# Rolling up five stages of a layer-stack kernel, and moving one addition of the retention from GpSimd to TensorE

## The chip, the cores and the metric

The kernel runs on one core of a Trainium2 chip. A core has TensorE (PE in the profile, its weight loads as PEld), VectorE (DVE), ScalarE (ACT), GpSimd (POOL) and SyncE (SP), which here only issues transfers from HBM to the on-chip memory. The metric is the device time of one execution in microseconds.

## The reference

The program computes three blocks on a sequence of 256 tokens and 1024 features, in float32: a block with three kinds of attention and a convolutional FFN, a block with stick-breaking and block attention and a SwiGLU FFN, and a block with retention and a SwiGLU FFN. What the change touches is this much of it: the two SwiGLU FFNs, the first block's FFN, and the group norm over each retention head.

```python
h = rmsnorm(x, ffn_pre_norm[l])                                   # stages "up", "down"
u = causal_depthwise_conv(h @ w_up[l], conv_w[l], conv_b[l])
gate, up = jnp.split(u, 2, axis=-1)
y = (jax.nn.gelu(gate, approximate=True) * up) @ w_down[l]
...
# the two later FFNs, SwiGLU: stages "gu0", "dn0" and "gu1", "dn1"
...
# retention (stage "ret_in"): 4 heads, 512 values each; every head's output is
# normalised over its 512 values, which needs their sum of squares per token
```

## The kernel before, in words

All activations lie transposed: 128 features on the partitions, 256 tokens along the free dimension, 8 such tiles for 1024 features. Every weight matrix is cut into chunks of up to 128 x 2048 elements. A chunk is loaded by SyncE into one of four raw slots; ScalarE rounds it to fp32r (`w_hi`, L802), VectorE computes the remainder (`w_lo`, L2219), each in two halves into one of two slots; and TensorE multiplies three times per tile (L1474 to L1476: hi x hi, lo x hi, hi x lo). So a chunk of the stages up, gu0 and gu1 is 16 tiles or 48 matmuls of 256 columns, and a chunk of dn0 and dn1 is 11 tiles or 33 matmuls. There are 22 chunks in up, gu0 and gu1 each, and 16 in dn0 and dn1 each. Finished chunks lie in two PSUM banks (`lin`); a bank is given free through the semaphores `lin_free`.

Each engine has its own instruction stream, written in the order in which it runs, and the streams meet only in semaphores. In gu0 ScalarE leaves the gate half of a chunk (L1330), GpSimd and VectorE form the products (L2585 reads the up half and gives the bank free), and VectorE in between multiplies pieces of a large conditioning matrix (L2323, with the accumulator read, and L2326, which writes a column of `mod`).

The helper `steps(eng, n, lead, tail, body)` runs a stage's chunks on an engine. Before the change it ignores `lead` and `tail` and calls `body(Step(c))` for every chunk, so all chunks are written out in the stream. The class `Step` can also carry a loop register `i`; its method `n(f)` then gives a value that grows by `f(j + 4) - f(j)` per trip, used for the semaphore values, the columns and the addresses.

In the retention, ScalarE squares the four 128-value pieces of a head's output (L1421, `sq`, 1024 columns). GpSimd adds the upper 512 columns to the lower (L762), and then columns 256 to 511 to columns 0 to 255 (L765). TensorE then sums over the partitions with two 128x1 matmuls (`ret_sums`, L2160), one for each half of the tokens, placed in the middle of a chunk. VectorE reads the sums (L2873).

Of the kernel before, what the change touches and what calls it, by code (L numbers as in the profile page):

```python
# [18 lines left out]
ALU = mybir.AluOpType  # L19

P = 128
S = 256
# [17 lines left out]
UNROLL = 4  # L40
# [144 lines left out]

def steps(eng, n, lead, tail, body):

    for c in range(n):
        body(Step(c))


# [22 lines left out]
def scaled_before(norm):  # L214

    return sum(norm_tiles(i) for i in range(norm))
# [24 lines left out]
def deferred_before(norm):  # L241
    return sum(i < norm for i in DEFERRED)


def additions(norm, n):

    if norm == PRE:
        return 0
    if norm in DEFERRED:
        return 5 if norm == L0F else 6  # L250
    return max(n - 1 - 3, 0)
# [28 lines left out]
def build(nc, dram):  # L280
    ctx = ExitStack()
    with ctx:
        def sb(name, n, dt=F32, parts=P):
            return ctx.enter_context(nc.sbuf_tensor(name, [parts, n], dt))

        def sem(name):
            return ctx.enter_context(nc.semaphore(name))
# [9 lines left out]
        ident, ones = sb("ident", P), sb("ones", S)  # L297
# [13 lines left out]
        def parts(table, end=ADA0 - D):  # L311
            at, out = 0, {}
            for name, n in table:
                out[name] = arena[:, at:at + n]
                at += n
            assert at <= end, (at, end)
            return out

        e0, a1, ff, a2, rt = parts(EARLY), parts(ATT1), parts(FFN), parts(ATT2), parts(RET, ARENA)
# [19 lines left out]
        ssum = sco[0][:, 0:6]  # L339
# [6 lines left out]
        def spread_bank(i, g):  # L346
# [36 lines left out]
        ret_rot, ret_s, ret_inner, v_centred, ret_o, ret_sq, ret_added, ret_ssum, ret_ms, ret_root, ret_diag, ret_rbc = (  # L383
            sem(n) for n in ("ret_rot", "ret_s", "ret_inner", "v_centred", "ret_o", "ret_sq", "ret_added", "ret_ssum", "ret_ms",
                             "ret_root", "ret_diag", "ret_rbc"))
# [17 lines left out]
        def v3(ap, n):  # L403
            return ap.rearrange("p (a b) -> p a b", a=n)
# [17 lines left out]
        for i, layer, which in ((L0, 0, 0), (L0F, 0, 3), (L1, 1, 0), (L1F, 1, 3)):  # L422
            NORM[i] = (x[:, :], e0["sq"], e0["y"],
                       lambda k, i=i: gscale[:, 8 * (L0, L0F, L1, L1F).index(i) + k:8 * (L0, L0F, L1, L1F).index(i) + k + 1],
# [11 lines left out]
        def rbc_copy(i):  # L436
            return arena[:, SETTLED_AT[i]:SETTLED_AT[i] + S]
# [5 lines left out]
        def z_cut(i, k, lo_, n=S):  # L443

            parts_ = Z_PARTS[i]
            first, _, at = parts_[0] if len(parts_) == 1 or k < parts_[0][1] else parts_[1]
            return Z_IN[i][lo_][:, bass.ds((k - first) * ZW + at, n)]
# [5 lines left out]
        def shifts(i, part):  # L453
            which = (L0, L0F, L1, L1F).index(i)
            at, (first, end, _) = 48 * (which // 2) + 24 * (which % 2), Z_PARTS[i][part]
            return mod[:, at + first:at + end].unsqueeze(2).to_broadcast([P, end - first, ZW - S])
# [14 lines left out]
        def settled_tile(i, c, b):  # L471
            return settled_chunk(i, c)[:, b * ZW:b * ZW + S]
# [220 lines left out]
        @block.gpsimd  # L693
        def _(pool):
            added = [0]

            def add_squares(i):

                sq, k0 = NORM[i][1], 0
                for n in NORM_GROUPS[i]:  # L700
                    acc = sq[:, k0 * S:(k0 + 1) * S]
                    for k in range(k0 + 1, k0 + 1 + additions(i, n)):
                        pool.wait_ge(sq_ready, scaled_before(i) + k + 1)
                        if k > k0 + 1:

                            pool.wait_ge(sq_added, added[0])
                        nc.gpsimd.tensor_tensor(acc, acc, sq[:, k * S:(k + 1) * S], ALU.add).then_inc(sq_added, 1)  # L707
                        added[0] += 1
                    k0 += n

            def hidden(step):
                j = step.j
                at, cut = S * (j % 2), bass.ds(step.n(lambda c: c * S), S)
                hid = ff["hid"][:, at:at + S]

                pool.wait_ge(gelu_ready, step.n(lambda c: c + 1))
                nc.gpsimd.tensor_tensor(hid, ff["u"][:, 2 * at + S:2 * at + 2 * S], ff["g"][:, at:at + S], ALU.mult)\
                    .then_inc(hid_ready, 1)
                pool.wait_ge(hid_hh, step.n(lambda c: c + 1))
                nc.gpsimd.tensor_tensor(hid_lo[:, cut], hid, hid_hi[:, cut].bitcast(F32), ALU.subtract).then_inc(hid_tiles, 1)  # L720

            def remainder(base):
                def one(step):
                    j = step.j
                    pool.wait_ge(hid_hh, step.n(lambda c: base + c + 1))
                    cut = bass.ds(step.n(lambda c: c * S), S)
                    nc.gpsimd.tensor_tensor(hid_lo[:, cut], ff["hid"][:, S * (j % 2):S * (j % 2) + S], hid_hi[:, cut].bitcast(F32),  # L727
                                            ALU.subtract).then_inc(hid_tiles, 1)
                return one

            pool.wait_ge(band_ready, 1)
            pool.dma_start(dram["band"], band).then_inc(band_out, 16)
            pool.wait_ge(band_out, 16)
            pool.dma_start(dram["band_rows"], dram["band_repeat"]).then_inc(band_out, 16)
            pool.wait_ge(band_out, 32)
            pool.dma_start(v3(a1["bias"], 8), dram["band_skew"]).then_inc(bias_in, 16)
            def settle(i):

                pool.wait_ge(rbc_copied, deferred_before(i) + 1)
                ph = PH[AHEAD[i]]  # L740
                for c in range(DEFERRED_CHUNKS):
                    for b in range(2):
                        if b == 0:
                            pool.wait_ge(first_left, DEFERRED_CHUNKS * deferred_before(i) + c + 1)
                        else:
                            pool.wait_ge(lin_free[(ph.unit0 + c) % 2], (ph.unit0 + c) // 2 + 1)
                        nc.gpsimd.tensor_tensor(settled_tile(i, c, b), settled_tile(i, c, b), rbc_copy(i), ALU.mult)\  # L747
                            .then_inc(settled, 1)

            for i in range(len(NORM_GROUPS)):  # L750
                if i != PRE and NORM_GROUPS[i]:
                    add_squares(i)
                if i in DEFERRED:
                    settle(i)
                if i in (L0F, L1F):

                    steps(pool, FT, 2, 0, remainder(FT if i == L0F else 2 * FT))
                if i == L1:

                    for h in range(RET_H):  # L760
                        pool.wait_ge(ret_sq, 2 * h + 2)
                        nc.gpsimd.tensor_tensor(rt["sq"][:, 0:512], rt["sq"][:, 0:512], rt["sq"][:, 512:1024], ALU.add)\  # L762
                            .then_inc(ret_added, 1)
                        pool.wait_ge(ret_added, 2 * h + 1)
                        nc.gpsimd.tensor_tensor(rt["sq"][:, 0:S], rt["sq"][:, 0:S], rt["sq"][:, S:2 * S], ALU.add).then_inc(ret_added, 1)  # L765
                if i == FFNPRE:

                    steps(pool, PH["up"].n, 2, 1, hidden)
                if i == FINAL:
                    pool.wait_ge(x_gains, DT)  # L770
                    pool.wait_ge(rbc_copied, len(DEFERRED) + 1)
                    for k in range(FINAL_SPLIT, DT):
                        cut = slice(k * S, (k + 1) * S)
                        nc.gpsimd.tensor_tensor(e0["y"][:, cut], e0["y"][:, cut], e0["sq"][:, 0:S], ALU.mult).then_inc(pool_tiles, 1)
# [696 lines left out]
        def _(pe):  # L1471
# [682 lines left out]
            def ret_sums(h):  # L2154


                pe.wait_ge(ret_inner, RET_H)
                pe.wait_ge(ret_added, 2 * h + 2)
                for r in range(2):
                    ins = nc.tensor.matmul(ssum[:, r:r + 1], rt["sq"][:, r * P:r * P + P], ones[:, 0:1],  # L2160
                                           start=r == 0, stop=r == 1, skip_group_check=True)
                ins.then_inc(ret_ssum, 1)

            def ret_spread(h):
# [980 lines left out]
```

## Time and profile before

| | us |
|---|---|
| median of 3 runs | 1054.75 (1052.81 to 1055.11) |
| the profiled execution | 1054.75 |
| its span, first to last instruction | 1053.0 |
| TensorE busy | 1027.0 |
| VectorE busy | 804.9 |
| ScalarE busy | 594.6 |
| GpSimd busy | 161.6 |

Busy means that at least one instruction of the engine was under way; matmuls overlap each other, so their durations add up to more than the span. Register instructions, waits and branches are not counted as busy. The stages lie in the span about as follows: up from 160 to 269 us, down to 331, gu0 from 460 to 589, dn0 to 652, gu1 from 850 to 982, dn1 to 1040.

### The profile page before, as it was taken

How to read it: one execution, taken by the hardware profiler on the slowest of the kernel's cores; microseconds unless marked ns; L12 is line 12 of the kernel's file. 1: busy time of each engine (PE TensorE's matmuls, PEld its weight loads, DVE VectorE, ACT ScalarE, POOL GpSimd, SP SyncE). 2: the span in 40 equal slices, each digit the busy share in tenths (PEclk: the TensorE clock that was granted, in tenths of full speed). 3: DMA queues.
4: the chain of work that ended last, by engine and by line, in shares of the span. 5: the costliest groups of instructions: out<-in, count | busy, mean ns of one | idle time of the engine just before them, and what ended most of it. 6: DMA issues, size and time to landing. Idle time of an engine off the chain costs nothing.

```text
span 1053.0 us, 19187 instructions
## 1 busy us (share of the span) xinstructions
PE 1027.0 (98%) x7842; PEld 975.0 (93%) x7842; DVE 804.9 (76%) x1380; ACT 594.6 (56%) x1029; POOL 161.6 (15%) x168
## 2 busy tenths in 40 slices
PE   7999999999999999999999999999999999999997
PEld 6987798999888997899999999998899999999997
DVE  5867789999997987588999688885668566674443
ACT  6686667666546675675444445543556466544443
POOL 0000033323201200024212001200110114111010
PEclk8999999999999999999999999999999999999999
DMA  9642336777695543157998788554444536774441
GB/s 369 248 143 98 103 131 227 301 273 284 256 391 228 165 152 125 74 207 278 375 370 340 283 326 306 170 193 160 126 155 142 218 122 226 278 278 150 166 166 40
DMA packets 33988, 227.49 MB, mean 216 GB/s; under 512 B 3779, under 2 KB 4076, under 8 KB 10220
## 3 DMA queue, kind: packets, MB, share of 16 engines
q1 hardware_dynamic: 33452, 223.63, 57.9%
q0 software_dynamic: 448, 2.63, 0.6%
q8 instruction: 62, 1.02, 0.4%
q14 instruction: 26, 0.21, 0.1%
HBM read 225.19 MB, written 2.63 MB: 216 GB/s over the span
## 4 chain that ended last, share of the span: by engine, by line
PE 80%; DVE 12%; ACT 5%; issue 1%; DMA 0%; POOL 0%; POOLq 0%; SPq 0%; ACTq 0%; DVEq 0%
PE psum L1474 20%; PE psum L1476 20%; PE psum L1475 20%; DVE w_lo L2219 5%; PE psum L1539 2%; PE psum L1542 2%; PE psum L1541 2%; PE psum L1883 2%; PE psum L1885 2%; PE psum L1884 2%; ACT w_hi L802 2%; DVE arena L2522 1%; DVE arena L2323 1%; DVE hid_lo L2304 1%; PE psum L2149 1%
## 5 line engine op out<-in xcount | busy, mean ns | idle before, releaser
L2219 DVE TENSOR_TENSOR w_lo<-raw,w_hi 128x1024 fp32r<-128x1024 f32 (+1 forms) x342 | 389.5, 1161 | 148.2 <-ACT w_hi L802 143.3
L802 ACT ACTIVATE w_hi<-raw 128x1024 fp32r<-128x1024 f32 (+1 forms) x342 | 335.4, 996 | 209.7 <-PE psum L1476 157.7
L1474 PE MATMUL psum<-h_hi,w_hi 128*128 128x256 f32 (+1 forms) x1144 | 325.5, 285 | 7.6 <-DVE w_lo L2219 3.0
L1475 PE MATMUL psum<-h_lo,w_hi 128*128 128x256 f32 (+1 forms) x1144 | 321.1, 281 | 0.0
L1476 PE MATMUL psum<-h_hi,w_lo 128*128 128x256 f32 (+1 forms) x1144 | 320.6, 280 | 0.0
L1474 PE MATMUL psum<-hid_hi,w_hi 128*128 128x256 f32 (+1 forms) x952 | 270.9, 285 | 0.6 <-DVE w_lo L2219 0.4
L1475 PE MATMUL psum<-hid_lo,w_hi 128*128 128x256 f32 (+1 forms) x952 | 268.1, 282 | 0.0
L1476 PE MATMUL psum<-hid_hi,w_lo 128*128 128x256 f32 (+1 forms) x952 | 268.1, 282 | 0.0
L1474 PEld LDWEIGHTS psum<-h_hi,w_hi 128*128 128x128 f32 x1144 | 215.3, 188 | 10.7 <-DVE w_lo L2219 5.4
L1475 PEld LDWEIGHTS psum<-h_lo,w_hi 128*128 128x128 f32 x1144 | 216.2, 189 | 0.7 <-issue 0.7
L1476 PEld LDWEIGHTS psum<-h_hi,w_lo 128*128 128x128 f32 x1144 | 215.9, 189 | 0.0
L1474 PEld LDWEIGHTS psum<-hid_hi,w_hi 128*128 128x128 f32 x952 | 179.4, 188 | 2.1 <-DVE w_lo L2219 1.2
L1475 PEld LDWEIGHTS psum<-hid_lo,w_hi 128*128 128x128 f32 x952 | 179.5, 189 | 0.0
L1476 PEld LDWEIGHTS psum<-hid_hi,w_lo 128*128 128x128 f32 x952 | 179.3, 188 | 0.0
L2323 DVE CUSTOM_DVE_ANT_0 arena<-arena 128x1024 f32<-128x1024 f32 x96 | 128.0, 1370 | 0.7 <-DMA arena<-in_ada 0.4
L707 POOL TENSOR_TENSOR arena<-arena 128x256 f32<-128x256 f32 x33 | 28.3, 857 | 427.7 <-ACT arena L1263 255.7
L1154 ACT ACTIVATE hid_hi<-arena 128x256 fp32r<-128x256 f32 x60 | 25.1, 418 | 100.2 <-DVE arena L2585 75.0
L727 POOL TENSOR_TENSOR hid_lo<-arena,hid_hi 128x256 fp32r<-128x256 f32 x44 | 41.9, 952 | 169.2 <-ACT hid_hi L1154 157.0
L747 POOL TENSOR_TENSOR arena<-arena 128x256 f32<-128x256 f32 x30 | 36.2, 1228 | 77.5 <-ACT arena L1052 64.7
L1883 PE MATMUL psum<-w_hi,hid_hi 128*128 128x512 f32 x88 | 34.8, 396 | 0.0
L1884 PE MATMUL psum<-w_hi,hid_lo 128*128 128x512 f32 x88 | 34.7, 395 | 0.0
L1885 PE MATMUL psum<-w_lo,hid_hi 128*128 128x512 f32 x88 | 34.7, 395 | 0.0
(294 smaller groups left out, 1215.7 us busy)
## 6 DMA issues: line engine op xcount, KB each, us to landing
arena<-in_ada SPq DMA_DIRECT2D x48, 1024.0 KB, 6.3
raw<-in_gu SPq DMA_DIRECT2D x44, 1024.0 KB, 6.9
raw<-in_ret_in SPq DMA_DIRECT2D x24, 1024.0 KB, 4.9
raw<-in_up SPq DMA_DIRECT2D x22, 1024.0 KB, 4.9
raw<-in_dn SPq DMA_DIRECT2D x32, 704.0 KB, 4.2
raw<-in_qkv SPq DMA_DIRECT2D x12, 1024.0 KB, 5.0
raw<-in_down SPq DMA_DIRECT2D x11, 1024.0 KB, 8.3
raw<-in_ret_o SPq DMA_DIRECT2D x8, 1024.0 KB, 4.8
```

What stands on the lines that cost most here:

```text
L707: nc.gpsimd.tensor_tensor(acc, acc, sq[:, k * S:(k + 1) * S], ALU.add).then_inc(sq_added, 1)
L727: nc.gpsimd.tensor_tensor(hid_lo[:, cut], ff["hid"][:, S * (j % 2):S * (j % 2) + S], hid_hi[:, cut].bitcast(F32), ALU.subtract).then_inc(h ...
L747: nc.gpsimd.tensor_tensor(settled_tile(i, c, b), settled_tile(i, c, b), rbc_copy(i), ALU.mult)\
L802: nc.scalar.activation(w_hi[chunk % SPLIT_SLOTS][:, a:b], raw[chunk % RAW_SLOTS][:, a:b], ACT.Copy)\
L1474: nc.tensor.matmul(out, w[0], hc, start=start, stop=False, skip_group_check=True)
L1475: nc.tensor.matmul(out, w[0], lc, start=False, stop=False, skip_group_check=True)
L1476: return nc.tensor.matmul(out, w[1], hc, start=False, stop=stop, skip_group_check=True)
L1883: nc.tensor.matmul(bank[:, :], hid_hi[:, t:t + P], whi[:, w], start=c == 0 and k == 0, stop=False, skip_group_check=True)
L1884: nc.tensor.matmul(bank[:, :], hid_lo[:, t:t + P], whi[:, w], start=False, stop=False, skip_group_check=True)
L1885: ins = nc.tensor.matmul(bank[:, :], hid_hi[:, t:t + P], wlo[:, w], start=False, stop=last and k == 1, skip_group_check=True)
L2219: tt(w_lo[s][:, a:b], raw[chunk % RAW_SLOTS][:, a:b], w_hi[s][:, a:b].bitcast(F32), ALU.subtract)\
L2323: ins = nc.vector.tensor_tensor_reduce(w, w, cond_silu, 1.0, 0.0, ALU.mult, ALU.add, sums[:, b:b + 1])
```

## The change

It has two parts. `steps` now writes out only the first `lead` chunks and what is left at the end; in between it puts four chunks (UNROLL) into a loop that runs `trips` times. On TensorE this gives 3 trips each in up, gu0, gu1 and dn0, and 2 in dn1. VectorE gets 3 trips in up and gu0 and 2 in dn0 and dn1; ScalarE 3 in up and gu0 and 2 in dn0, gu1 and dn1; SyncE and GpSimd have such loops as well. The order of the work on each engine is the same. In the second part GpSimd's second addition per head goes, and TensorE sums four pieces with four 128x1 matmuls.

```diff
 def steps(eng, n, lead, tail, body):
 
-    for c in range(n):
+    lead = min(lead, n)
+    trips = (n - lead - tail) // UNROLL
+    if trips < 2:
+        trips = 0
+    for c in range(lead):
+        body(Step(c))
+    if trips:
+        with eng.Fori(0, trips) as i:
+            for j in range(UNROLL):
+                body(Step(lead + j, i))
+    for c in range(lead + trips * UNROLL, n):
         body(Step(c))
...
                         nc.gpsimd.tensor_tensor(rt["sq"][:, 0:512], rt["sq"][:, 0:512], rt["sq"][:, 512:1024], ALU.add)\
                             .then_inc(ret_added, 1)
-                        pool.wait_ge(ret_added, 2 * h + 1)
-                        nc.gpsimd.tensor_tensor(rt["sq"][:, 0:S], rt["sq"][:, 0:S], rt["sq"][:, S:2 * S], ALU.add).then_inc(ret_added, 1)
...
-                pe.wait_ge(ret_added, 2 * h + 2)
-                for r in range(2):
-                    ins = nc.tensor.matmul(ssum[:, r:r + 1], rt["sq"][:, r * P:r * P + P], ones[:, 0:1],
-                                           start=r == 0, stop=r == 1, skip_group_check=True)
+                pe.wait_ge(ret_added, h + 1)
+                for f in range(2):
+                    for r in range(2):
+                        ins = nc.tensor.matmul(ssum[:, r:r + 1], rt["sq"][:, f * S + r * P:f * S + r * P + P], ones[:, 0:1],
+                                               start=f == 0 and r == 0, stop=f == 1 and r == 1, skip_group_check=True)
```

TensorE's stream where the loop of gu0 begins, now. The loop's first chunk starts behind the branch; before, the matmuls stand here without anything between them.

```order
L1484 MATMUL psum<-h_hi,w_lo 128x256
L195 UNCONDITIONAL_BRANCH
L195 ISA
L408 ISA [waits split_ready]
L1482 MATMUL psum<-h_hi,w_hi 128x256 [waits lin_free1]
L1483 MATMUL psum<-h_lo,w_hi 128x256
```

And where the same loop ends, 192 matmuls later, now:

```order
L1484 MATMUL psum<-h_hi,w_lo 128x256
L195 REGISTER_ALU
L195 COMPARE_AND_BRANCH
L1482 MATMUL psum<-h_hi,w_hi 128x256 [waits lin_free1,split_ready]
```

Two register instructions and a branch have come between the matmuls, and some register instructions stand between tiles inside the loop.

VectorE's stream in gu0, one chunk, before:

```order
L2585 TENSOR_TENSOR arena<-psum,arena 128x256 [waits hid_tiles,gelu_ready]
L2323 ISA arena,ada_sums<-arena 128x1024 [waits ada_in1]
L2323 ISA ada_sums 128x1
L2323 ISA arena,ada_sums<-arena 128x1024
L2323 ISA ada_sums 128x1
L2326 TENSOR_TENSOR mod<-ada_sums,cols 128x2 [waits ada_sum]
L2219 TENSOR_TENSOR w_lo<-raw,w_hi 128x1024 [waits hi_ready] x2
```

The same chunk in the loop, now (an ISA without names computes registers):

```order
L2227 REGISTER_ALU
L2228 TENSOR_TENSOR w_lo<-raw,w_hi 128x1024 [waits hi_ready]
L2591 REGISTER_ALU
L2593 REGISTER_ALU [waits gelu_ready]
L2594 TENSOR_TENSOR arena<-psum,arena 128x256 [waits hid_tiles]
L2332 ISA arena,ada_sums<-arena 128x1024 [waits ada_in1]
L2332 ISA ada_sums 128x1
L2332 ISA arena,ada_sums<-arena 128x1024
L2332 ISA ada_sums 128x1
L2334 REGISTER_ALU
L2335 ISA [waits ada_sum]
L2335 TENSOR_TENSOR mod<-ada_sums,cols 128x2
```

The operations are the same; between them stand register instructions for the semaphore values and the column of `mod`, and the wait for `ada_sum` is now at a register instruction ahead of the last operation.

TensorE's sums of a retention head, before and then now:

```order
L1542 MATMUL psum<-w_hi,hid_lo 128x512
L2160 MATMUL psum<-ones,arena 128x1 [waits ret_added,ret_inner]
L2160 MATMUL psum<-ones,arena 128x1
L1539 MATMUL psum<-w_hi,hid_hi 128x512 [waits lin_free0]
L1541 MATMUL psum<-w_lo,hid_hi 128x512
```

```order
L1550 MATMUL psum<-w_hi,hid_lo 128x512
L2169 MATMUL psum<-ones,arena 128x1 [waits ret_added,ret_inner]
L2169 MATMUL psum<-ones,arena 128x1 x3
L1547 MATMUL psum<-w_hi,hid_hi 128x512 [waits lin_free0]
L1549 MATMUL psum<-w_lo,hid_hi 128x512
```

Two more 128x1 matmuls stand between the chunk's two halves.

## Rows read from the trace of the kernel before

**Rows 1.** The page: busy time, share of the span, instructions; then granted clock by slice.
```profile
PE 1027.0 (98%) x7842; PEld 975.0 (93%) x7842; DVE 804.9 (76%) x1380; ACT 594.6 (56%) x1029; POOL 161.6 (15%) x168
...
PE   7999999999999999999999999999999999999997
...
PEclk8999999999999999999999999999999999999999
```

**Rows 2.** Windows, TensorE: length, busy (instructions), clock, DMA share, GB/s.
```profile
200.00:269.00 69.00, 69.00 (x577) 1.00 0.71 267
269.00:331.00 62.00, 62.00 (x269) 1.00 0.89 351
500.00:590.00 90.00, 88.80 (x754) 1.00 0.91 345
590.00:652.00 62.00, 62.00 (x525) 1.00 0.87 323
870.00:980.00 110.00, 110.00 (x936) 1.00 0.63 228
980.00:1040.00 60.00, 60.00 (x509) 1.00 0.40 134
```

**Rows 3.** The same view for VectorE, in the stage up.
```profile
200.00:269.00 69.00, 64.24 (x103) 1.00 0.71 267
```

**Rows 4.** TensorE's waits, 200 to 1040 us: total us, times, longest.
```profile
PE psum L1474 <- DVE w_lo L2219: 1.7, 3, 0.9
PE psum L1474 <- DVE arena L2585: 1.2, 1, 1.2
PE psum L2170 <- DVE arena L2893: 0.5, 1, 0.5
PE psum L1905 <- DVE diag L2300: 0.3, 1, 0.3
```

**Rows 5.** Timeline of VectorE in gu0: start, duration, engine, line, operation.
```profile
560.94 2.35 DVE L2219 TENSOR_TENSOR w_lo<-raw,w_hi 128x1024 fp32r<-128x1024 f32 x2
563.21 0.42 DVE L2585 TENSOR_TENSOR arena<-psum,arena 128x256 f32<-128x256 f32 x1
...
564.69 0.08 DVE L2323 DVE_READ_ACCUMULATOR2_ANT ada_sums<- 128x1 f32 x1
564.69 1.75 DVE L2323 CUSTOM_DVE_ANT_0 arena<-arena 128x1024 f32<-128x1024 f32 x1
...
566.49 0.16 DVE L2326 TENSOR_TENSOR mod<-ada_sums,cols 128x2 f32<-128x2 f32 x1
566.56 1.22 DVE L2219 TENSOR_TENSOR w_lo<-raw,w_hi 128x1024 fp32r<-128x1024 f32 x1
```

**Rows 6.** Timeline of ScalarE at the same place.
```profile
560.27 0.36 ACT L1330 ACTIVATE arena<-psum 128x256 f32<-128x256 f32 x1
...
563.99 2.00 ACT L802 ACTIVATE w_hi<-raw 128x1024 fp32r<-128x1024 f32 x2
565.89 0.36 ACT L1330 ACTIVATE arena<-psum 128x256 f32<-128x256 f32 x1
```

**Rows 7.** DMA queues, the one that carries TensorE's code: packets, MB, share.
```profile
q8 instruction: 62, 1.02, 0.4%
```

**Rows 8.** DMA issues: KB each, median us from issue to landing.
```profile
raw<-in_gu SPq DMA_DIRECT2D x44, 1024.0 KB, 6.9
...
out<-arena SPq DMA_DIRECT2D x4, 256.0 KB, 2.6
...
ident<-in_ident SPq DMA_DIRECT2D x1, 64.0 KB, 4.6
```

**Rows 9.** Timeline of the retention's second head.
```profile
753.63 1.60 POOL L765 TENSOR_TENSOR arena<-arena 128x256 f32<-128x256 f32 x1
...
755.83 0.53 PEld L2160 LDWEIGHTS psum<-ones,arena 128*128 128x128 f32 x4
```

**Rows 10.** One line of the kernel, L2160: weight loads, ns least, median, most.
```profile
L2160 PEld LDWEIGHTS psum<-ones,arena x16: 187/192/193, 741.0 to 786.0; 128*128 128x128 f32 x16
```

## The prediction

> **What bounds the kernel now.** I read the busy shares and the slices first: TensorE is busy for 1027.0 of 1053.0 us, its granted clock is at nine tenths or more in every slice but the first [rows 1]. Then the windows of the five stages that the change rolls up. TensorE is busy for every microsecond of five of the six windows, and for 88.80 of 90 in the other [rows 2]; the list of TensorE's waits from 200 to 1040 us has four entries with 3.7 us in all [rows 4]. So in these stages the end is set by how fast TensorE is fed and runs. Anything that VectorE, ScalarE, GpSimd or the transfers lose is free until it makes TensorE wait. A gu chunk of 48 matmuls takes 48 x 110/936 = 5.64 us, a dn chunk of 33 takes 33 x 62/525 = 3.90 us [rows 2].
>
> How much cover there is must be read at one place. In gu0, chunks end at 560.2 and 565.8: ScalarE reads the finished bank (L1330) at 560.27 and 565.89 [rows 6]. The bank that the chunk starting at 565.8 needs is given free by VectorE's product L2585, which ends at 563.21 + 0.42 = 563.63 [rows 5]. TensorE's instruction stream can't have passed that wait before 563.63, and TensorE shows no gap up to 565.8, so it held about 2.2 us of queued matmuls. A stall of the stream costs only what exceeds this 2.2 us. The same rows show that VectorE has no idle time in gu0: from one w_lo pair (560.94) to the next (566.56) is 5.62 us, all filled, against TensorE's 5.64 [rows 5].
>
> **Part 1, loops in place of straight code.** TensorE gets five loops: up, gu0 and gu1 with three trips each, dn0 with three, dn1 with two. The taken backward branches are 2+2+2+2+1 = 9. A gu or up trip has 192 matmuls; each is a weight load and a multiply, as the profile counts them, so 384 instructions, and with the register and branch instructions about 398. A dn trip has 132 matmuls, about 276 instructions. The work of TensorE's arrays is the same, matmul for matmul. What is new is the way its code arrives. Queue q8 moved 62 packets, 1.02 MB [rows 7]: 16.4 KB each, one for every 15684/62 = 253 TensorE instructions. Straight code is fetched in blocks of about 256 instructions, one after another, and the full windows show that this costs nothing now. Both bodies are longer than one block, so a backward branch goes one or two blocks back, and that block may have to be fetched again while the stream stands.
>
> The trace shows no such refetch, so its price is bounded by transfers. The code packet itself is 0.4% of 16 engines' span over 62 packets, 0.004 x 16 x 1053/62 = 1.1 us each [rows 7], and a landing adds its issue and completion: the quickest landing in the kernel is the output's, 2.6 us, a small 64 KB load at the start took 4.6 and the weights in the busy gu stages 6.9 [rows 8]. Less the 2.2 us of cover an edge costs 0.4 to 4.7 us, nine of them 4 to 42 us; and nothing at all if the block is still there. A code packet is small like the first two, so I take the middle of 2.6 and 4.6, 3.6 us: 1.4 exposed, nine edges **12.6 us**. By the Trainium skill, page "Runtime: NRT & Kernel Launch", section "Instruction fetch mechanics", prefetch is purely sequential and a taken branch to a block outside the two held ones waits for a fetch; the trace agrees on the sequential blocks, and shows no branch. The same section gives TensorE room for 2048 instructions, by which every body here would stay and the sum would be Part 2 alone.
>
> A branch that finds its code costs sequencer time only. The page "Advanced Engine Details and Errata", section "Control Flow Timing", has 108 ns for a compare-and-branch, and no run here shows it. From rows: the smallest instruction that the trace has, VectorE's read of its accumulator, is 0.08 us [rows 5]; a branch of ten times that is still under the 2.2 us of cover, so zero. The other loops: SyncE's loads have four raw slots and land in 6.9 us against 5.64 a chunk; ScalarE is busy for only 56% of the span [rows 1]; both are costed at nothing behind TensorE. If that cover went (a fetch of 3.6 us on ScalarE in gu0), VectorE would start w_lo late by 3.6 less the 0.6 us between the end of ScalarE's w_hi (563.99 + 2.00) and the next w_lo (566.56), and TensorE by a further 2.2 less: 0.8 us for an edge [rows 5, 6].
>
> VectorE needs more care. In gu0 its loop has 59 instructions where four chunks did 32 before, 27 more per trip, 6.75 per chunk, and one of them (the address of the mod column) now waits for the sum ahead of the last operation. Bounds: nothing if its sequencer is ahead, or all exposed at the 0.08 us of the smallest DVE row, 0.54 us per chunk; 12 chunks 6.5 us, less the 2.2 us lead, 4.3 us at most. I take nothing: register instructions stand between operations of 0.3 to 1.8 us [rows 5]. In up VectorE is busy for 64.24 of 69 us [rows 3], 4.8 us free over 12 chunks.
>
> **Part 2, the sums of the retention.** Four GpSimd additions (L765) go. In the tightest of the four heads it ends at 753.63 + 1.60 = 755.23, and TensorE's weight loads for the sums start at 755.83 [rows 9]; no wait of TensorE for GpSimd stands in the list [rows 4]. Gain on the path: nothing, at best the 0.6 us if that head was held there. In exchange TensorE sums four pieces per head in place of two. Its two 128x1 matmuls appear as four weight loads in 0.53 us, with 0.19 us for one [rows 9, 10], so a step is (0.53 - 0.19)/3 = 0.11 us; four more make 0.45 us per head, on the engine that never waits there, **1.8 us** for four heads. From below -0.6, the gain above; from above 4 x 0.53 = 2.1.
>
> Sum: 12.6 + 1.8 = 14.4 us. The profiled execution took 1054.75 us, its span 1053.0 with 1.75 us around it, and it is the median of the runs shown. Forecast: **1069.2 us**.
>
> **Rivals.**
> A (forecast, 0.53): refetch on each TensorE edge, 1060 to 1084. For: bodies of 1.1 and 1.6 blocks; the steady one-for-one fetching. Against: the trace can't tell whether older blocks are kept.
> B (0.22): older blocks are kept, or the queue covers the whole fetch. Then only Part 2 is left, 1054.75 + 1.8 = 1056.6. For: TensorE's stretch of 2.2 us is almost the 2.6 us of the quickest landing. Against: the other landings.
> C (0.13): branches are covered but VectorE becomes the bound in gu0. For: it has no idle microsecond there, and 0.02 us per chunk to spare. 1056.6 + 4.3 = 1061. Against: only one wait per chunk has a register instruction right behind it.
> D, the other side (0.04): matmul spacing is set by delivery of instructions, and code that is in place already delivers faster. The price: 2388 matmuls run inside the loops. A 512-wide matmul takes 62.0/269 = 230 ns, so 256 columns alone are 115 ns; the spacing is 119.6 in up, 117.5 in gu and 118 in dn [rows 2]. If the difference went: 576 x 4.4 + 1152 x 2.3 + 660 x 2.8 ns = 7 us, 1054.75 + 1.8 - 7 = 1049.6. It decides if the spacing inside a loop drops in trips two and three. Against: half of the 512-wide time is nearly all of it, so columns set the pace.
> E (0.08): each edge costs a full busy landing, or two fetches in a row: 9 x 4.7 = 42 us, 1099. TensorE idle this long could also lose its clock; the slices show it below full only at the start [rows 1].
>
> **How the numbers follow.** About 2 us (0.2%) is what a measurement can tell from no change. A, C and E are slower: 0.74; B lies at +1.8, of it 0.18 same and 0.04 slower; D is faster: 0.04. So 0.04 / 0.18 / 0.78. The range 1056 to 1084 holds A whole, B and C, and leaves D and E out, 0.12, with a little of A's upper end.
>
> **What would show it.** The profile after: TensorE idle with the reason "issue" or none, nine times, one after every 192 matmuls (22.6 us) in up and gu, every 132 (15.6 us) in dn, 1 to 2 us each. Queue q8: 6 x 192 + 3 x 132 = 1548 matmuls are no longer written out, 3096 instructions or 12 blocks, so near 50 packets if blocks are kept, and 65 or more if each edge fetches again. Part 2: eight records of the 128x1 matmul per head and 0.45 us more before TensorE's next chunk. C would show as TensorE waiting for w_lo late in gu0 and not at the edges. The forecast is wrong if the loops have no gaps (B), or if gaps are longer than 3 us (E).

## The result, and the profile of the changed kernel

The changed kernel takes 1061.09 us (median of 5 runs, 1060.51 to 1062.09), the kernel before 1055.11 in the same comparison: ratio 1.0057 (95% interval 1.0046 to 1.0069), 6 us slower. I had forecast 1069.2, for a reason that turns out not to exist. The execution that was profiled took 1060.25 us, its span 1058.4.

The page of the changed kernel: busy time by engine, the queue that carries code, and the shares of the chain of waits that ended last.

```profile
PE 1031.8 (97%) x7858; PEld 978.4 (92%) x7858; DVE 807.0 (76%) x1380; ACT 595.1 (56%) x1029; POOL 156.1 (15%) x164
...
PEclk8999999999999999999999999999999999999999
...
q8 instruction: 50, 0.82, 0.3%
...
PE 73%; DVE 18%; ACT 6%; issue 3%; DMA 1%; DVEq 0%; POOL 0%; SPq 0%; POOLq 0%; ACTq 0%
```

The same last line of the kernel before:

```profile
PE 80%; DVE 12%; ACT 5%; issue 1%; DMA 0%; POOL 0%; POOLq 0%; SPq 0%; ACTq 0%; DVEq 0%
```

The clock is as in [rows 1]. Code packets fell from 62 [rows 7] to 50. VectorE now holds 18% of the chain and not 12%. Six per cent of the span would be over 60 us, so the share doesn't give the price of the loss; it points to the engine. The windows say in which stage. TensorE, the columns as in [rows 2]:

```profile
200.00:269.00 69.00, 68.15 (x569) 1.00 0.69 266
269.00:331.00 62.00, 62.00 (x271) 1.00 0.88 348
500.00:590.00 90.00, 88.21 (x729) 1.00 0.89 339
590.00:652.00 62.00, 62.00 (x524) 1.00 0.85 323
870.00:980.00 110.00, 110.00 (x934) 1.00 0.61 222
980.00:1040.00 60.00, 60.00 (x508) 1.00 0.44 145
```

Between 500 and 590 us, in gu0, TensorE starts 25 matmuls fewer than in [rows 2], 25 x 0.118 = 2.9 us. In up it is idle for 0.85 us where it was never idle. In dn0 and dn1, where TensorE and VectorE have loops too, and in gu1, where TensorE has one and VectorE has none, it stays busy throughout. Setting the start of the same matmul side by side in the two traces gives the account: 0.5 us gained ahead of up, then up +0.65, down -0.2, from there to gu0 +0.3, gu0 +3.1, dn0 nothing, the retention +1.85, the product after it +0.6 (not from the change: there TensorE only places its matmuls 120.0 ns apart and not 118.7, see the last section), gu1 and dn1 nothing: 5.8 us in all.

TensorE's waits from 200 to 1040 us, which answer to [rows 4]:

```profile
PE psum L1482 <- DVE arena L2594: 1.8, 3, 1.3
PE psum L1482 <- DVE w_lo L2228: 1.8, 3, 1.1
PE psum L1482 <- DVE arena L2570: 0.8, 3, 0.3
PE psum L2179 <- DVE arena L2902: 0.5, 1, 0.5
PE psum L1913 <- DVE diag L2309: 0.3, 1, 0.3
```

L2594 is the product (L2585 before) and L2570 the last step of the convolution's taps in up; both free a bank for TensorE. They make 2.6 us here, 1.2 before.

VectorE's timeline in gu0, across one backward branch of its loop (between `mod` at 557.62 and w_lo at 558.17) and one chunk within a body. The bracket is the idle time ahead and what ended it.

```profile
557.37 0.08 DVE L2332 DVE_READ_ACCUMULATOR2_ANT ada_sums<- 128x1 f32 x1
557.62 0.16 DVE L2335 TENSOR_TENSOR mod<-ada_sums,cols 128x2 f32 x1 [0.18 <-DVE ada_sums L2332]
558.17 2.36 DVE L2228 TENSOR_TENSOR w_lo<-raw,w_hi 128x1024 fp32r<-128x1024 f32 x2 [0.39 <-issue]
560.45 0.42 DVE L2594 TENSOR_TENSOR arena<-psum,arena 128x256 f32<-128x256 f32 x1
...
563.61 0.08 DVE L2332 DVE_READ_ACCUMULATOR2_ANT ada_sums<- 128x1 f32 x1
563.87 0.16 DVE L2335 TENSOR_TENSOR mod<-ada_sums,cols 128x2 f32 x1 [0.18 <-DVE ada_sums L2332]
563.98 2.36 DVE L2228 TENSOR_TENSOR w_lo<-raw,w_hi 128x1024 fp32r<-128x1024 f32 x2
...
566.26 0.42 DVE L2594 TENSOR_TENSOR arena<-psum,arena 128x256 f32<-128x256 f32 x1
```

Two things are new beside [rows 5]. The addition to `mod` starts 0.26 us after the accumulator read (563.87 - 563.61), where it took 0.11 (566.49 - 566.38): its wait for ada_sum now stands at the register instruction that computes the addition's address, ahead of the addition. And after a backward branch VectorE stands for another 0.39 us. From product to product is 566.26 - 560.45 = 5.81 us against 5.62 before. A chunk costs TensorE 48 x 0.1178 = 5.65: VectorE has become the slower one by 0.16 us, and by more at a branch.

That TensorE follows it at once is seen at the other branch of gu0. First TensorE, then VectorE, both of the changed kernel:

```profile
536.77 0.28 PE L1484 MATMUL psum<-h_hi,w_lo 128*128 128x256 f32 x1
537.26 0.39 PE L1482 MATMUL psum<-h_hi,w_hi 128*128 128x256 f32 x1 [0.21 <-DVE arena L2594]
```

```profile
534.51 2.36 DVE L2228 TENSOR_TENSOR w_lo<-raw,w_hi 128x1024 fp32r<-128x1024 f32 x2 [0.41 <-issue]
536.79 0.42 DVE L2594 TENSOR_TENSOR arena<-psum,arena 128x256 f32<-128x256 f32 x1
```

The product ends at 536.79 + 0.42 = 537.21, the chunk starts at 537.26. Two matmuls start 0.49 us apart where 0.12 is usual. Of the 2.2 us of "queued work" that I had predicted as cover, nothing is seen here.

The retention's sums, one head, answering to [rows 9]; 0.98 us for eight weight loads, against 0.53 for four:

```profile
759.55 0.98 PEld L2169 LDWEIGHTS psum<-ones,arena 128*128 128x128 f32 x8
```

### The profile page after: what moved, and what is told of

The parts are those of the page before. It is cut to its first block, busy times and chain, and to the rows that moved or that the text cites. A ratio compares the mean times of both kernels' runs of the same rounds, so it can differ in the third digit from the quotient of the medians.

```text
span 1058.4 us, 20275 instructions
## 1 busy us (share of the span) xinstructions
PE 1031.8 (97%) x7858; PEld 978.4 (92%) x7858; DVE 807.0 (76%) x1380; ACT 595.1 (56%) x1029; POOL 156.1 (15%) x164
## 4 chain that ended last, share of the span: by engine, by line
PE 73%; DVE 18%; ACT 6%; issue 3%; DMA 1%; DVEq 0%; POOL 0%; SPq 0%; POOLq 0%; ACTq 0%
PE psum L1482 18%; PE psum L1484 17%; PE psum L1483 17%; DVE w_lo L2228 7%; DVE arena L2332 4%; PE psum L1547 2%; PE psum L1550 2%; PE psum L1549 2%; PE psum L1891 2%; PE psum L1893 2%; PE psum L1892 2%; ACT w_hi L810 2%; DVE arena L2531 1%; DVE hid_lo L2313 1%; PE psum L2157 1%
## 5 line engine op out<-in xcount | busy, mean ns | idle before, releaser
L1162 ACT ACTIVATE hid_hi<-arena 128x256 f32 (+1 forms) x60 | 25.1, 418 | 104.2 <-DVE arena L2594 78.9
L737 POOL TENSOR_TENSOR hid_lo<-arena,hid_hi 128x256 f32 (+1 forms) x44 | 38.1, 866 | 176.2 <-ACT hid_hi L1162 163.8
```

## Experiments

The theory after the result: VectorE's loop costs the 3 us of gu0, by the wait held as an instruction and by the branch; TensorE's loops cost nothing; the new sums cost 1.8 us. The rivals: the loops of the other engines, or looped instructions as such.

Each was compared with the kernel before on the same chip: median 1055.89 us for the first four, 1055.12 for the next four, 1054.49 for the last three. Repeated executions of the kernel before spread over 3.8 us in the first set, which the last section comes back to, so where less than 1 us matters the ratio with its interval decides.

**e1_address_first.** The changed kernel, with the addresses computed ahead of the wait.

```
 def piece(step, f):
     ...
+    to, bias = step.n(lambda c: 2 * f(c)), step.n(lambda c: o + 2 * f(c))
     dve.wait_ge(ada_in[slot], ...)
     ...
-    tt(mod[:, bass.ds(step.n(lambda c: 2 * f(c)), 2)], sums, cols[:, ...
+    tt(mod[:, bass.ds(to, 2)], sums, cols[:, bass.ds(bias, 2)],
```

> The changed kernel with one edit on VectorE: the address of the mod column (and of its bias) is computed ahead of the wait for the two sums, so that the wait stands at the last operation itself again; loops and the sums of the retention stay as changed. Theory: in the loop of gu0 VectorE, which had no idle time, loses 0.18 us per chunk at that wait and some 0.3 us at a branch because its instruction stream is held there; this makes the 3.1 us that the changed kernel loses in gu0. Then the chunk period in gu0 goes back to 5.62 to 5.66 us, the idle time before L2335 to 0.03 us, and the time to 1058.0 (1057.3 to 1058.8). Rival, register instructions and branches as such cost it: the period stays at 5.8 us and the time at 1061.

Measured: 1061.31 us, ratio 1.0047 (1.0034 to 1.0061). The edit is no test of the theory: in its trace the addition to `mod` still stands 0.18 us idle (at 564.47), with the wait at a register instruction of the addition's own line, so moving the expression in the program did not move that instruction. My 1058.0 was missed for that reason. It serves as a second measurement of the changed kernel. A real version is e5.

**e2_sums_only.** The kernel before with only the retention's part of the change (one GpSimd addition in place of two, four 128x1 matmuls in place of two).

> The kernel before with the second part of the change alone: GpSimd's second addition gone, four 128x1 matmuls per head in place of two. Theory: 0.45 us per head on an engine that never waits there, +1.8 us, 1056.9. Rival, GpSimd's addition held TensorE in some head: +1.2 us or less. Rival, the sums cost only because of the loops: +0.

Measured: 1055.85 us, ratio 1.0004 (0.9994 to 1.0014). In the trace the same matmul is 1.78 us further back after the retention than ahead of it, as expected. In the medians at most 1.5 us of it is seen, so by them alone the theory's 1.8 is missed.

**e3_pe_loops.** The kernel before with loops on TensorE alone.

```
-    steps(pe, ...)
+    rolled_steps(pe, ...)     # the changed kernel's steps()
```

> The kernel before with loops on TensorE alone (all five), everything else written out. Theory: the 50 code packets of the changed kernel show that blocks stay on the chip, and no gap stands at a backward branch, so +0 (1054.3 to 1055.9), 50 packets on q8. The forecast's step (1.4 us per edge) would give +12.6.

Measured: 1054.92 us, ratio 0.9992 (0.9983 to 1.0001). Its code queue:

```profile
q8 instruction: 50, 0.82, 0.3%
```

No gap stands at any of the nine backward branches, and 50 packets say that nothing was fetched twice. My forecast's main term, 12.6 us, is 0.

**e4_dve_loops.** The same edit, for VectorE alone.

> The kernel before with loops on VectorE alone (up, gu0, dn0, dn1). Theory: all of the loops' cost is VectorE's wait at a register instruction in gu0 and its branches: +3.1 to +4 us, 1058.2 to 1059.1, with a chunk period of 5.8 us in gu0. Rival, the loss in gu0 needs ScalarE's loop as well: under +2 us.

Measured: 1059.08 us, ratio 1.0029 (1.0020 to 1.0038), 3.1 us, with up +1.0 and gu0 +3.1 by the trace. VectorE's timeline has the changed kernel's two marks:

```profile
557.79 0.16 DVE L2344 TENSOR_TENSOR mod<-ada_sums,cols 128x2 f32 x1 [0.18 <-DVE ada_sums L2341]
558.34 2.36 DVE L2237 TENSOR_TENSOR w_lo<-raw,w_hi 128x1024 fp32r<-128x1024 f32 x2 [0.39 <-issue]
```

Here TensorE's code is straight, and it waits all the same: the loss is made on VectorE. From 514 us on, TensorE's chunks of gu0 take about 5.82 us in this trace, 6.27 and 6.24 at the two branches, and each starts 0.15 us after the end of the product that frees its bank.

**e5_wait_at_add.** The changed kernel, with the wait as a condition of the addition.

```
-    dve.wait_ge(ada_sum, step.n(lambda c: f(c) + 1))
+    done = step.n(lambda c: f(c) + 1)
+    if step.i is not None:
+        done = dve.lower_val(done)
     tt(mod[:, ...], sums, cols[:, ...],
-       ALU.add).then_inc(ada_out, 1)
+       ALU.add)._wait_ge(ada_sum, done).then_inc(ada_out, 1)
```

> The changed kernel, but in VectorE's piece the wait on ada_sum is a condition of the addition itself and no instruction of its own in front of it; loops, registers and branches stay. Theory (VectorE paces gu0 and the separate wait is what it loses within a loop body): idle before the addition to mod falls from 0.18 us to about 0.03, chunks of gu0 within a body come back to about 5.65 us, only the two backward branches of gu0 keep 0.4 to 0.5 us each, so that TensorE is behind by about 1 us at the end of gu0 instead of 2.75: about 1059.3 us. Rival (reading the address from a register costs the time, or every looped instruction does): idle stays at 0.18 us, 1061.1 us.

Measured: 1058.64 us, ratio 1.0028 (1.0017 to 1.0040). The intervals of this and of the changed kernel (1.0046 to 1.0069) don't touch: 0.0029 x 1055 = 3 us came back; against e1's 1.0047 (1.0034 to 1.0061) it is 2, and those two intervals overlap. VectorE in gu0, across a backward branch and then within the body:

```profile
555.34 0.08 DVE L2332 DVE_READ_ACCUMULATOR2_ANT ada_sums<- 128x1 f32 x1
555.45 0.16 DVE L2337 TENSOR_TENSOR mod<-ada_sums,cols 128x2 f32 x1
555.99 2.36 DVE L2228 TENSOR_TENSOR w_lo<-raw,w_hi 128x1024 fp32r<-128x1024 f32 x2 [0.38 <-issue]
558.27 0.42 DVE L2596 TENSOR_TENSOR arena<-psum,arena 128x256 f32<-128x256 f32 x1
...
563.91 0.42 DVE L2596 TENSOR_TENSOR arena<-psum,arena 128x256 f32<-128x256 f32 x1
```

The addition follows the read by 0.11 us as before, the chunk is 563.91 - 558.27 = 5.64 us, and on VectorE only the branch's 0.38 is left. The registers and the looped instructions are the same in number (in the trace of gu0, 51 and 21 register instructions of the two kinds in both kernels), so they weren't the cost.

What is left of the loss lies for the most part in up and not in gu0. In gu0 the first branch holds TensorE up by about 0.4 us (its chunk starts at 535.69, 0.05 us after the end of the product); from there on it spaces its matmuls 120.0 ns apart and needs 5.76 us a chunk (see the last section), and the second branch costs 0.03 us. In e11, with that spacing in the whole loop of gu0, every chunk takes 5.76 us and neither branch costs anything. In up, TensorE's waits from 195 to 269 us in e5 are:

```profile
PE psum L1482 <- DVE arena L2572: 0.6, 2, 0.4
```

I had expected the remaining loss, 1 us, at the two branches of gu0; the 1059.3 us is near, the place is half wrong.

**e6_loops_only.** The kernel before with loops on every engine, the sums as before.

> The kernel before with the loops on every engine, the retention's sums as before. Theory (loops cost what VectorE's cost alone, 1059.1 us measured for those; TensorE's cost nothing): 1059.3 us, 1.8 under the whole change. Rival (the engines' loops add up, refetches of one delaying another): 1061 us or over, and the sums then cost nothing.

Measured: 1059.60 us, ratio 1.0038 (1.0027 to 1.0050), as the theory said (1059.3); 0.0019, or 2.0 us, below the whole change.

**e7_loops_not_dve.** Loops on every engine but VectorE.

> Loops on TensorE, ScalarE, SyncE and GpSimd, VectorE in straight code. Theory (VectorE's is the one that counts): 1055.5 to 1056, no change. Rival (ScalarE's loops or the transfers issued from a loop cost too): 1057 or over, with ScalarE's or SyncE's work ending TensorE's waits.

Measured: 1056.31 us, ratio 1.0006 (0.9996 to 1.0017). That is 0.3 us over the theory's range, with the kernel before at 1055.12. A cost of the other loops of up to 1.8 us isn't excluded; 3 us is. In its trace up is as long as before to 0.01 us and TensorE waits for nothing in it; gu0 and dn0 are 1.7 and 0.7 us longer than before, as in e3 and e8, by the wider spacing of the matmuls (last section).

**e8_one_more_addition.** The kernel before, with one small addition more on VectorE in each of 16 chunks of gu0, which doubles the suspected kind of cost without any loop.

```
     if c < ph.n:
         pieces(ph.name, step)
+        if ph.name == "gu0" and 4 <= c <= 19:
+            tt(more_[:, 2 * (c % 4):2 * (c % 4) + 2], cols[:, 0:2], cols[:, 0:2], ALU.add)
```

> The kernel before with one more 128x2 addition (about 0.16 us) on VectorE in each of the 16 chunks of gu0 that load conditioning weights. Theory (VectorE has 0.1 to 0.6 us of lead over TensorE in gu0 and then sets its pace): 16 x 0.19 = 3.0 less the lead of 0.1 at the start and less 16 x 0.03 us per chunk by which TensorE is the slower one: +2.2 to +2.9 us, 1057.8 to 1058.6. Rival (my reading in the prediction, 2.2 us of queued matmuls as cover): +0.3 to 0.8 at most.

Measured: 1054.89 us, ratio 0.9999 (0.9988 to 1.0009). Missed, by my pricing: I took the row's duration for its cost. VectorE in this run:

```profile
564.96 0.16 DVE L2327 TENSOR_TENSOR mod<-ada_sums,cols 128x2 f32<-128x2 f32 x1
565.04 0.15 DVE L2789 TENSOR_TENSOR more<-cols 128x2 f32<-128x2 f32 x1
565.11 2.35 DVE L2220 TENSOR_TENSOR w_lo<-raw,w_hi 128x1024 fp32r<-128x1024 f32 x2
```

From start to start the new operation takes 0.07 us, not 0.16. The chunk became 5.70 us, 0.05 over TensorE's 5.65, 0.8 us in 16 chunks; and in this execution TensorE itself took 5.76. So the dose was too small to tell the theories apart.

**e9_three_additions.** The same with three additions (a loop `for e in range(3)` around the last line).

> The kernel before with three more 128x2 additions on VectorE in each of the 16 chunks of gu0 with conditioning weights. One of them lengthened a chunk by 0.08 us only (start to start) and so stayed under TensorE's own 5.65 to 5.76 us. Theory (VectorE paces gu0 as soon as its chunk is longer than TensorE's): the chunk becomes 5.625 + 3 x 0.08 = 5.865 us; against TensorE's 5.65 that is 16 x 0.21 = 3.4, less the lead of 0.1 us: about 1058 us (1057 where TensorE spaces its matmuls 120.0 ns apart and needs 5.76 itself). TensorE's chunks start as VectorE's product ends. Rival (2.2 us of queued matmuls as cover, as I had predicted): 16 x 0.21 - 2.2, 1 us or less, and TensorE waits for nothing until the last chunks.

Measured: 1057.49 us, ratio 1.0029 (1.0019 to 1.0040), 3.1 us. VectorE:

```profile
562.24 0.16 DVE L2327 TENSOR_TENSOR mod<-ada_sums,cols 128x2 f32<-128x2 f32 x1
562.32 0.29 DVE L2790 TENSOR_TENSOR more<-cols 128x2 f32<-128x2 f32 x3
562.53 2.35 DVE L2220 TENSOR_TENSOR w_lo<-raw,w_hi 128x1024 fp32r<-128x1024 f32 x2
564.80 0.41 DVE L2586 TENSOR_TENSOR arena<-psum,arena 128x256 f32<-128x256 f32 x1
```

With the product ahead of it at 558.98 the chunk is 5.82 us, and 16 x (5.82 - 5.65) = 2.7 us, less the lead of 0.1 us. By the trace gu0 loses 3.0 us, TensorE's chunks take about 5.84 us from 501 us on, and each starts 0.14 to 0.15 us after the product ahead of it has ended. This shows without any loop that VectorE's chunk time sets gu0's pace. A cover of 2.2 us would have left 1 us or less.

**e10_long_loops.** The kernel before, with loops of keep-busy matmuls ahead of its first work. Only its trace is of use.

```
     pe.wait_ge(busy_ready, 1)
+    for n in (200, 700, 1200):
+        with pe.Fori(0, 3):
+            keep_busy(n)
     keep_busy(16)
```

> The kernel before, with three loops of three turns each ahead of its first matmuls on TensorE: 200, 700 and 1200 matmuls of 128x256 in the body, that is 400, 1400 and 2400 instructions (with the weight loads). It prices a refetch of code where there is one. Theory: bodies that fit what the chip keeps of TensorE's code refetch nothing, as the 398 instructions of the changed kernel: no gap at the backward branches of 400. The code is longer by 4200 instructions, 269 KB, 16 to 17 packets of 16 KB, so the instruction queue shows 62 + 17 = 79 packets if nothing is fetched twice; if the 2400 are fetched anew on each of the two returns, 2 x 9.4 = 19 more (98) and a gap of 0.5 to 7 us at each of them (bounds from landings of the kernel before); if the 1400 are too, 11 more again (109). Rival (what I predicted): every backward branch costs about 1.4 us whatever the body's length.

Measured: one execution of 1814.79 us. First the window that holds the loop of 700, then TensorE's timeline at the two backward branches of the loop of 1200, and the code queue:

```profile
75.00:327.00 252.00, 252.00 (x2102) 1.00 0.00 0
```

```profile
472.25 0.88 PE L1552 MATMUL psum<-busy 128*128 128x256 f32 x6
474.69 0.74 PE L1552 MATMUL psum<-busy 128*128 128x256 f32 x4 [1.57 <-issue]
```

```profile
618.08 0.88 PE L1552 MATMUL psum<-busy 128*128 128x256 f32 x6
620.61 0.62 PE L1552 MATMUL psum<-busy 128*128 128x256 f32 x3 [1.65 <-issue]
```

```profile
q8 instruction: 101, 1.65, 0.4%
```

A body of 1400 instructions has no idle moment in 252 us; one of 2400 stands for 1.57 and 1.65 us idle at exactly its two returns (1.85 and 1.93 us from matmul to matmul), with 101 packets where code fetched once would make 79. That code is fetched again there is concluded from the 22 packets more and the two gaps; 19 had been expected. The bodies of this change, of at most about 398 instructions, are far too short for it.

**e11_loops_repaired.** e5 with the retention's sums as before: loops everywhere, the wait in the addition.

> Loops on all engines, the wait inside VectorE's addition, and the retention's two GpSimd additions and two matmuls as before. Theory: the parts add, so 1058.6 (the same with the new sums) less 1.8 = 1056.9 us, which is the kernel before plus VectorE's branches (some 0.4 to 0.5 us at the two of gu0 and at those of up). Rival (the sums cost nothing measurable, as 1.0004 for them alone could be read): 1058.6 us.

Measured: 1056.94 us, ratio 1.0021 (1.0012 to 1.0031). The absolute figure is met, but the kernel before was 0.6 us quicker in this set; by the ratio it is 2.2 us over it, and 0.0007, 0.7 us, under e5. In its trace TensorE waits for VectorE's taps three times in up, 0.9 us in all.

## Why the prediction was wrong

**The cover of 2.2 us (wrong, and the first mistake).** I read the end of a chunk from ScalarE's L1330 at 565.89 [rows 6], as if ScalarE had been waiting for TensorE. Its row has no idle time and no releaser. The row above says why it starts there: ScalarE's own w_hi runs from 563.99 for 2.00 us, and L1330 is next in its queue. TensorE's chunk starts much earlier. The kernel before, TensorE, the first matmuls of a chunk (found by counting 48 at a time):

```profile
564.17 0.28 PE L1474 MATMUL psum<-h_hi,w_hi 128*128 128x256 f32 x1
564.29 0.28 PE L1475 MATMUL psum<-h_lo,w_hi 128*128 128x256 f32 x1
```

The bank it needs comes free at 563.63 [rows 5], so VectorE led by 0.54 us at this chunk. Over the stage the distance from the product's end to the chunk's start grows from 0.14 us (at 501.9) and 0.25 (at 507.6) to 0.63; where TensorE is held, as in e4 and e9, it is 0.15, so the slack is 0.1 to 0.5 us. I had the two numbers that mattered, 5.62 and 5.64 us a chunk, and set a cover at least four times too large beside them.

**The refetch, nine times 1.4 us (wrong).** The step that failed is that the earlier block "may have to be fetched again", on which rival A had 0.53 and rival B 0.22. Nothing is fetched again (e3: 50 packets, no gap, ratio 0.9992). My own test for it, near 50 packets if blocks are kept and 65 or more if not, came out as B. The price of 1.4 us is near the 1.57 and 1.65 us that e10 shows, but by luck: it was a landing of 3.6 us, chosen as a middle, less the cover of 2.2 us that had been misread. And it belongs to longer bodies: one of 1400 instructions doesn't pay it, one of 2400 does (e10). By the Trainium skill, page "Runtime: NRT & Kernel Launch", section "Instruction fetch mechanics", TensorE has room for 2048 instructions, and e10 agrees. The same section's warning that only two blocks are held is not what the runs show: 1400 instructions are more than five blocks and were kept. I had both statements and gave the chance to the wrong one.

**VectorE in gu0 (the step that mattered; valued at 0, measured at 1.4 to 3.1 us).** My bounds were 0 and 0.54 us a chunk; I took 0, because register instructions stand between long operations. That is true of the registers (e5: with them, 5.64 us a chunk), and not of the one wait: made an instruction of its own, it costs 0.15 us a chunk, since the address of the next operation is computed only once the wait is over. Twelve chunks of 0.15 to 0.18 make 2 us; two branches at 0.39 and 0.41 make 0.8; against a lead of 0.1 to 0.5 nearly all of it arrives. How much that is depends on what it is set against: gu0 takes 113.2 us with VectorE's loops (the change and e4), and without them 110.1 where TensorE spaces its matmuls 117.8 ns apart (before) but 111.8 where it spaces them 120.0 apart (e7). So the loss is 3.1 us against the one and 1.4 against the other. All of VectorE's loops together cost 3.1 us in the medians, with 2.1 to 4.0 (e4). Rival C named the mechanism and came out at 1061, the time measured; I gave it 0.13, because "only one wait per chunk has a register instruction right behind it". One was enough. Its number was partly luck: it had 4.3 us for gu0 alone, of which 3.1 at most came, and nothing for up. Its sign was half right: TensorE waits for the product and not for w_lo, and at VectorE's branches as well.

**VectorE in up (called covered by 4.8 us).** TensorE was idle there for 0.85 us. An average over a stage isn't cover at each place: three times there the taps (L2570) free a bank too late, by 0.3 us at most. In the kernel before, the taps end 1.7 us ahead of one chunk and only 0.7 ahead of the next, in turn; the backward branches fall to the tight ones. The price is clearest in e4, whose up has the spacing of the kernel before: 113.6 us against 112.6, two chunks of 6.25 and 6.23 us among chunks of 5.76. In the change's own trace part of this is hidden, for there some chunks of up happen to have the closer spacing. At these branches VectorE stands for 0.24 to 0.26 us, and the pair of w_lo behind them takes 2.90 us where the kernel before has 2.35; why was not traced.

**ScalarE, SyncE, GpSimd at 0.** Holds within what can be told: 0.6 us, with -0.4 to 1.8 (e7, which has TensorE's loops as well).

**Part 2, 1.8 us (right in the trace, open in the medians).** Eight weight loads take 0.98 us for 0.53, the 0.45 per head that was worked out, and the traces shift by 1.8 to 1.9 us across the retention in all four runs that have the new sums (the change, e1, e2, e5) and by 0.0 to 0.1 in those that don't (e3, e4, e6 to e9, e11). In the medians the same part is worth 0.4 (e2), 2.0 (the change against e6) and 0.7 us (e5 against e11), each with an uncertainty of about 1. No gain from GpSimd's missing addition shows in the trace.

**The sum.** VectorE's loops 3.1, the others 0.6, the sums 0.4 to 2.0: 4.1 to 5.7 us, against 6.0 measured with 4.9 to 7.3. Which of the parts is a little larger stays open. In my forecast 12.6 + 1.8 + 0.

**Rivals D and E.** The spacing inside loops didn't fall, and no edge cost a landing of TensorE's code. But D's price was misread too: the 119.6 ns that I took for a property of up is one execution's; in e2 and e8, whose TensorE code there is that of the kernel before, up's chunks take 5.65 us, 117.8 ns a matmul.

## What to carry to other kernels

Where two engines have the same time per chunk, the profile's question isn't which is busy but by how much one leads the other; read it as the difference between when a bank is freed and when the chunk that needs it starts, and take a reader's start for the end of a chunk only if its row names a releaser. Before code is rolled up, look on the engine without slack for waits whose next operation has a computed address: a wait that was part of the operation becomes an instruction, and giving the wait to the operation itself took back 2 to 3 us of 6 here. Price a small operation from start to start and not by its row: VectorE's 128x2 addition cost 0.07 us where its row shows 0.16. And before a stage's length in one trace is set against another's, see whether TensorE's spacing is the same in both.

## What the runs showed of the hardware

**A small operation costs less than its duration.** 0.07 us from start to start for a row of 0.16 us, in e8 and e9.

**The spacing of matmuls takes one of two values.** With all inputs ready, TensorE places the 128x256 matmuls of up and gu0 117.8 ns apart in some stretches and 120.0 in others; in dn0 the two are 118.7 and 120.0. In the stretches looked at it keeps one value until something holds it up, if only for 0.03 us. Which one holds differs between executions. Windows of TensorE in up and gu0, the kernel before and then e8, whose TensorE work is the same:

```profile
205.00:225.00 20.00, 20.00 (x169) 1.00 0.80 310
512.00:532.00 20.00, 20.00 (x172) 1.00 0.98 377
```

```profile
205.00:225.00 20.00, 20.00 (x172) 1.00 0.76 301
512.00:532.00 20.00, 20.00 (x169) 1.00 0.98 372
```

The counts include the matmuls already under way at a window's start. All four windows are at the full granted clock (1.00), the DMA shares are nearly the same (0.80 and 0.76 in up, 0.98 in both in gu0), and one execution has the slower value in up, the other in gu0. What that makes of a stage is read from the starts of the matmuls, from a stretch's first to the first behind it (us; up and gu0 without their first three chunks, dn0 whole):

| run | up | gu0 | dn0 |
|---|---|---|---|
| before | 112.6 | 110.1 | 62.7 |
| e2, no loops | 111.0 | 110.1 | 62.7 |
| e3, TensorE's loops | 112.6 | 111.7 | 63.4 |
| e7, all but VectorE's | 112.6 | 111.8 | 63.4 |
| e8, one addition | 111.0 | 111.8 | 63.4 |
| e9, three additions | 112.6 | 113.1 | 62.7 |
| e4, VectorE's loops | 113.6 | 113.2 | 63.4 |
| the change | 113.2 | 113.2 | 62.7 |
| e5, wait repaired | 112.7 | 111.6 | 63.4 |
| e11, wait repaired, old sums | 113.2 | 111.8 | 63.4 |

So the slower value makes up 1.6 us longer, gu0 1.7 and dn0 0.7. Executions of one kernel spread by as much and more, which is why single traces must be compared stage by stage, and why 1.8 us in a trace can be 0.4 in medians. That the two values cause the spread is argued from these traces, not tested; what selects one was not found.

**A backward branch on VectorE** leaves it idle for 0.36 to 0.41 us in gu0 and dn0, and for 0.23 to 0.26 in up (gu0 and dn0 in the change, e4 and e5; up in e1, e4, e5 and e11), each time behind the short addition to `mod`. On TensorE, which is busy there, it cost nothing that can be seen (e3: nine of them, ratio 0.9992).
